# Expert chunks of one whole matrix: w1 or w3 in one load of 16 KB runs, multiplied 256 columns at a time

## The chip, the cores and the metric

The kernel runs on one core of one Trainium2 chip, in one launch. The metric is the device time in microseconds. Before the change three runs took 1033.55, 1036.56 and 1037.19 us, median 1036.56. A core has five engines that run their own instruction streams: TensorE (PE, with weight loads shown apart as PEld), VectorE (DVE), ScalarE (ACT), GpSimd (POOL) and SyncE (SP). Here SP issues nearly all loads from main memory; 16 DMA engines carry them out. All data is fp32; a matmul of fp32 operands shows as two records in the profile, one of fp32r operands (a rounded high part or its remainder) as one.

## The reference

256 tokens of width 1024 pass through two hybrid layers. The first ends in a mixture of 32 experts, the part that the change touches:

```
gl = h @ w_group + b_group;  g_idx = argmax(gl)              # 4 groups of 8 experts
el = (h @ w_expert) of that group + b_expert[g_idx]
vals, idx = top_k(softmax(el), 2); weights = g_w * vals / sum(vals)
for every expert e and the tokens x sent to it:
    y = (silu(x @ w1[e]) * (x @ w3[e])) @ w2[e]              # w1, w3: 1024 x 512, w2: 512 x 1024
out[token] += weight * y
```

Before it come two attention branches (Fox and differential) with gates, behind it a second hybrid layer with attention, a short convolution and their projections. Each of w1, w3 and w2 of one expert has 524288 numbers, 2.097 MB, so the experts together have 201.3 MB.

## The kernel before

**Stages.** The first layer's attention and projections take the span up to about 235 us, the experts 236 to 696 us, the second layer the rest.

**Experts.** An expert works on up to 64 slots for tokens. Four experts make a batch. A one-hot matrix (`PmR`) picks the tokens of a batch: for each of the eight blocks of 128 rows of the width, `gather(b, j)` multiplies the token rows (in a high and a low fp32r part, `XShR` and `XSlR`) by it, and VectorE copies the result out of the bank into `xe`, blocks 0 to 3 in one area and blocks 4 to 7 in another. Batch 0's gathers stand around expert 0, later ones are spread, two an expert. The products with w1 and w3 have the tokens as the stationary operand, 64 columns wide, so the array is split: output rows 0 to 63 of a bank take the first half of the 512 hidden columns (h = 0), rows 64 to 127 the other (h = 1). In the bank, columns 0 to 255 belong to w1 and 256 to 511 to w3. ScalarE applies Silu to the first, VectorE multiplies it by the second, TensorE transposes the result, and `down(e)` multiplies by w2, after the first half of the next expert. Every two experts `scatter` adds the outputs to the tokens in four banks.

**Loads.** A chunk of weights is 16 KB a partition, 2.097 MB. An expert has three: "a" has rows k = 0 to 3 of the eight that a partition holds, of w1 and of w3; "b" has rows 4 to 7 of both; "d" is w2. Each chunk is two DMAs of 1 MB with runs of 8 KB (line 246 builds them, line 839 in `load` issues them), and both raise the same semaphore, `landed`. The order of chunks is a0, b0, a1, d0, b1, a2, d1, b2 and so on; they go in turn into eight slots, five in `ring` and three in `arena`. Before it issues a load, SP waits in `released` until the slot's last chunk was used: for "a" by the semaphore `half`, which TensorE raises behind the first eight matmuls of an expert, for "b" and "d" by the bank's `full`. SP and its queue thus run as far ahead as TensorE frees slots.

**TensorE's order in an expert** (lines 1204 to 1257): chunk "a" in eight matmuls of 512 columns (four blocks, two halves; the 512 are 256 of w1 and 256 of w3, side by side in the chunk's two parts); `down` of the expert before; for expert 0 alone the gathers of blocks 4 to 7; at odd experts a scatter; chunk "b" in eight matmuls; two gathers of the next batch; the transposes. Before a block's matmul TensorE waits in `emptied` for VectorE's copy of that block, and before a gather in `may_write` for the bank that it writes.

**A branch.** The second 16 experts are written twice, in the two sides of a branch on `flag` (some expert has over 64 tokens, or not); TensorE reads the flag between experts 15 and 16. With these inputs it takes the side without overflow.

The names that the prediction uses: line 783 is the helper of every matmul, 839 the loads, 1302 to 1308 VectorE's helpers (1305 copies gathered tokens out), 2060 ScalarE's Silu, one an expert. In the changed file lines 783 and 839 are 782 and 838.

Of the kernel before, what the change touches and what calls it, by code (L numbers as in the profile page):

```python
# [22 lines left out]
SLOTS = 64  # L23
# [62 lines left out]
def bass_two_hybrid_blocks(nc, t, out):  # L86
    x_d, out_d = t["x"][0], out[0]
    with ExitStack() as ctx:
# [101 lines left out]
        ab = sm(224, 24)  # L190
# [49 lines left out]
        def expert_chunk(e, tag, what):  # L240

            if what == "d":
                w2 = t["w2"][0, e].rearrange("(g p c) n -> p g c n", g=2, c=2)
                return (tag, what, e), (w2[:, 0], w2[:, 1])
            k = 0 if what == "a" else 4
            return (tag, what, e), tuple(t[w][0, e].rearrange("(p k) n -> p k n", k=8)[:, k:k + 4, :] for w in ("w1", "w3"))

        def expert_chunks(tag):

# [47 lines left out]
        def space(nm):  # L297
            s = slot_of[nm]
            return ring[:, s * CH:s * CH + CH] if s < RING else area((60, 76, 102)[s - RING], CH)
# [482 lines left out]
        def mm(pe, o, l, r, start, stop):  # L782
            return pe.e.matmul(o, l, r, start=start, stop=stop)  # L783
# [362 lines left out]
        def experts_pe(pe, eng, r, P, S, lo, hi):  # L1146
# [4 lines left out]
            def gather(b, j):  # L1151
                u = P.of["g", r, b, j]
                may_write(pe, u)
                pe.wait_ge(S["select"], NB * g + b + 1)
                pe.wait_ge(s_xlow, 3)
                pe.wait_ge(s_xlow_dve, 1)
                for n in range(NT):
                    for x in (XShR, XSlR):
                        last = mm(pe, banks[u.bank][:, 0:256], x[:, n, j * 128:j * 128 + 128], PmR[:, b % 2, n, :],
                                  n == 0 and x is XShR, n == 1 and x is XSlR)  # L1160
                if b == 0 and j == 7:
                    last = slot_factors(0, banks[u.bank])
                last.then_inc(u.full, 1)
# [40 lines left out]
            for e in range(lo, hi):  # L1204
                b, k = divmod(e, EB)
                u = P.of["h", r, e]
                bank = banks[u.bank]
                for half in "ab":
                    may_write(pe, u)
                    pe.wait_ge(*landed[tag, half, e])  # L1210
                    w13 = space((tag, half, e)).rearrange("p (m k n) -> p m k n", m=2, k=4)
                    for j4 in range(4):
                        j = j4 + (4 if half == "b" else 0)
                        emptied(pe, P.of["g", r, b, j])
                        for h in range(2):
                            last = mm(pe, bank[64 * h:64 * h + 64, :].rearrange("p (m n) -> p m n", m=2),
                                      xe[b % 2][j // 4][:, j4, SLOTS * k:SLOTS * k + SLOTS], w13[:, :, j4, 256 * h:256 * h + 256],
                                      j == 0, j == 7)
                    if half == "a":
                        last.then_inc(S["half"], 1)  # L1220
                        if e:
                            down(e - 1)
                        if e == 0:
                            for j in range(4, 8):
                                gather(0, j)
                        if e > 2 and e % 2:
                            scatter((e - 3) // 2)
                    else:
                        last.then_inc(u.full, 1)
                if b + 1 < NB:  # L1230
                    gather(b + 1, 2 * k)
                    gather(b + 1, 2 * k + 1)
                if r in (0, 3) and e >= 28:
                    sp = P.of["spread", r, e - 28]
                    may_write(pe, sp)
                    pe.wait_ge(S["dg"], e - 27)
                    for i in range(4):
                        last = mm(pe, banks[sp.bank][:, 128 * i:128 * i + 128], ones[:, :], DG[i], True, True)
                    last.then_inc(sp.full, 1)
                if k == 2:  # L1240
                    w = P.of["w", r, b]
                    may_write(pe, w)
                    pe.wait_ge(s_identr, 1)
                    for p in range(2):
                        for n in range(NT):
                            last = mm(pe, banks[w.bank][:, 256 * p + 128 * n:256 * p + 128 * n + 128],
                                      PmR[:, b % 2, n, 128 * p:128 * p + 128], identR[:, :], True, True)
                    last.then_inc(w.full, 1)
                x = P.of["hT", r, e]
                may_write(pe, x)  # L1250
                emptied(pe, u)
                for c in range(2):
                    last = eng.transpose(banks[x.bank][:, 128 * c:128 * c + 128], Hb[e % 2][:, c:256:2], ident[:, :])  # L1253
                if k == 3 and b + 1 < NB:
                    last = slot_factors(b + 1, banks[x.bank])
                last.then_inc(x.full, 1)
# [1163 lines left out]
```

## Time and profile before

| | |
|---|---|
| runs | 1033.55, 1036.56, 1037.19 us |
| profiled execution | 1036.57 us, span 1034.8 us |
| mean granted TensorE clock | 0.985 of full |
| PE busy | 991.7 us (96%), 6369 matmul records |
| PEld busy | 697.8 us (67%) |
| DVE, ACT, POOL busy | 391.9, 377.1, 120.8 us |
| loads of expert weights | 192 DMAs of 1 MB (120 into ring, 72 into arena) |
| moved | 307.95 MB, mean 298 GB/s |

The span is the time from the first to the last instruction on the core. Busy PE is not PE at its peak: matmuls are pipelined, and their ends are modelled. Twice the same number of columns takes twice as long in the array, and the granted clock says at which share of its full clock the array runs in a stretch. An idle time has a releaser behind it: what ended it. "issue" stands where the profile shows nothing that was waited for. The rates by slice (40 equal parts of the span, 25.87 us each) show how full the queues are.

### The profile page before, as it was taken

How to read it: one execution, taken by the hardware profiler on the slowest of the kernel's cores; microseconds unless marked ns; L12 is line 12 of the kernel's file. 1: busy time of each engine (PE TensorE's matmuls, PEld its weight loads, DVE VectorE, ACT ScalarE, POOL GpSimd, SP SyncE). 2: the span in 40 equal slices, each digit the busy share in tenths (PEclk: the TensorE clock that was granted, in tenths of full speed). 3: DMA queues.
4: the chain of work that ended last, by engine and by line, in shares of the span. 5: the costliest groups of instructions: out<-in, count | busy, mean ns of one | idle time of the engine just before them, and what ended most of it. 6: DMA issues, size and time to landing. Idle time of an engine off the chain costs nothing.

```text
span 1034.8 us, 14930 instructions
## 1 busy us (share of the span) xinstructions
PE 991.7 (96%) x6369; PEld 697.8 (67%) x6369; DVE 391.9 (38%) x750; ACT 377.1 (36%) x612; POOL 120.8 (12%) x81
## 2 busy tenths in 40 slices
PE   7999999999999999979999999998999999999996
PEld 6988789975344434333344443348989999999995
DVE  3445446844222112121222211117334444774475
ACT  4445655641111111111111111216445555554443
POOL 1110021020000000000000000002321111341122
PEclk9999999999999999998999999999999999999998
DMA  8974386788999999999999999998545544445401
GB/s 270 347 277 147 125 319 252 284 324 337 421 422 421 419 421 421 421 420 420 422 421 421 421 421 421 421 404 297 201 166 186 187 167 167 163 164 198 148 1 41
DMA packets 84038, 307.95 MB, mean 298 GB/s; under 512 B 6609, under 2 KB 13170, under 8 KB 59386
## 3 DMA queue, kind: packets, MB, share of 16 engines
q1 hardware_dynamic: 80178, 302.16, 74.4%
q10 hardware_dynamic: 3784, 4.73, 1.4%
q8 instruction: 53, 0.87, 0.4%
q14 instruction: 23, 0.19, 0.1%
HBM read 305.82 MB, written 2.63 MB: 298 GB/s over the span
## 4 chain that ended last, share of the span: by engine, by line
PE 80%; DVE 6%; SPq 4%; DMA 3%; ACT 3%; issue 2%; POOL 1%; ACTq 0%; DVEq 0%
PE bank L783 78%; SPq L839 4%; DMA arena<-in_w 3%; DVE arena L1308 2%; DVE arena L1305 2%; ACT arena L2060 1%; PE bank L1253 1%; DVE wR L1302 1%; DMA arena<-in_rows 1%; PE bank L994 1%; DVE arena L1302 1%; POOL wR L2258 1%; ACT wR L1883 0%; DVE hTR L1302 0%; ACT arena L2113 0%
## 5 line engine op out<-in xcount | busy, mean ns | idle before, releaser
L783 PE MATMUL bank<-hTR,wR 128*128 128x256 f32 x2520 | 316.7, 286 | 4.5 <-DVE hTR L1308 1.3
L783 PEld LDWEIGHTS bank<-hTR,wR 128*128 128x128 f32 x2520 | 308.1, 193 | 8.5 <-issue 4.2
L783 PE MATMUL bank<-ring,arena 128*64 128x512 f32 (+2 forms) x1056 | 228.9, 600 | 8.0 <-issue 6.8
L1883 ACT ACTIVATE wR<-ring 128x1024 fp32r<-128x1024 f32 x161 | 168.3, 1054 | 111.1 <-PE bank L783 109.4
L1302 DVE TENSOR_TENSOR wR<-ring,wR 128x1024 fp32r<-128x1024 f32 x126 | 157.7, 1258 | 132.8 <-ACT wR L1883 132.5
L783 PE MATMUL bank<-arena 128*64 128x512 f32 (+7 forms) x778 | 165.5, 529 | 1.4 <-DVE small L1434 0.7
L783 PEld LDWEIGHTS bank<-ring,arena 128*64 128x64 f32 (+2 forms) x1056 | 69.9, 135 | 140.6 <-issue 136.9
L1308 DVE SCALAR_TENSOR_TENSOR arena<-bank,small,arena 128x256 f32<-128x256 f32 x32 | 15.5, 484 | 346.4 <-ACT arena L2060 346.4
L2031 ACT ACTIVATE arena<-bank,small 64x512 f32<-64x512 f32 x62 | 42.4, 684 | 280.7 <-PE bank L783 280.4
L2258 POOL TENSOR_TENSOR wR<-ring,wR 128x1024 fp32r<-128x1024 f32 x35 | 85.5, 2442 | 325.1 <-ACT wR L1883 325.1
L783 PEld LDWEIGHTS bank<-arena 128*64 128x64 f32 (+4 forms) x778 | 63.7, 148 | 85.5 <-issue 78.1
L2246 POOL TENSOR_TENSOR small<-small,mhalf 128x1 f32<-128x1 f32 (+1 forms) x12 | 7.2, 601 | 481.0 <-DVE small L1308 476.6
L783 PE MATMUL bank<-wR,hTR 128*128 128x512 f32 x192 | 45.2, 393 | 0.0
L2060 ACT ACTIVATE arena<-bank,small 128x256 f32<-128x256 f32 x32 | 15.2, 475 | 81.9 <-PE bank L783 81.9
L783 PEld LDWEIGHTS bank<-PmR,XShR 128*128 128x128 f32 x128 | 25.1, 196 | 24.2 <-issue 23.5
L783 PEld LDWEIGHTS bank<-wR,hTR 128*128 128x128 f32 x192 | 35.6, 188 | 8.1 <-issue 0.8
L783 PE MATMUL bank<-PmR,XShR 128*128 128x256 f32 x128 | 36.2, 314 | 0.4 <-DVE small L1494 0.3
L783 PE MATMUL bank<-PmR,XSlR 128*128 128x256 f32 x128 | 32.8, 287 | 0.0
L1305 DVE TENSOR_SCALAR arena<-bank,col 128x256 f32<-128x256 f32 x64 | 28.1, 476 | 4.8 <-PE bank L783 4.7
L1302 DVE TENSOR_TENSOR arena<-arena 128x512 f32<-128x512 f32 (+5 forms) x36 | 21.4, 603 | 10.8 <-ACT arena L2190 9.8
L1302 DVE TENSOR_TENSOR arena<-bank,arena 128x512 f32<-128x512 f32 (+2 forms) x30 | 19.6, 664 | 15.1 <-PE bank L783 12.8
L783 PEld LDWEIGHTS bank<-PmR,XSlR 128*128 128x128 f32 x128 | 25.2, 197 | 0.0
(209 smaller groups left out, 825.0 us busy)
## 6 DMA issues: line engine op xcount, KB each, us to landing
ring<-in_w SPq DMA_DIRECT2D x120, 1024.0 KB, 20.3
arena<-in_w SPq DMA_DIRECT2D x72, 1024.0 KB, 19.5
ring<-in_w_in SPq DMA_DIRECT2D x29, 2048.0 KB, 8.6
ring<-in_w_ada SPq DMA_DIRECT2D x6, 2048.0 KB, 7.9
ring<-in_w_o SPq DMA_DIRECT2D x2, 2048.0 KB, 12.3
ring<-in_w_o_attn SPq DMA_DIRECT2D x2, 2048.0 KB, 7.9
ring<-in_w_o_conv SPq DMA_DIRECT2D x2, 2048.0 KB, 8.6
ring<-in_w_out SPq DMA_DIRECT2D x2, 2048.0 KB, 8.1
```

Source lines behind the costliest of these rows:

```text
L783: return pe.e.matmul(o, l, r, start=start, stop=stop)
L839: e.e.dma_start(to[:, at_:at_ + k * n].rearrange("p (k n) -> p k n", k=k), part).then_inc(landed[nm][0], 16)
L994: last = eng.transpose(banks[u.bank][:, 128 * c:128 * c + 128], P[:, 128 * c:128 * c + 128], ident[:, :])
L1253: last = eng.transpose(banks[x.bank][:, 128 * c:128 * c + 128], Hb[e % 2][:, c:256:2], ident[:, :])
L1302: return eng.tensor_tensor(o, a, b, op)
L1305: return eng.tensor_scalar(o, a, s1, s2, op0) if op1 is None else eng.tensor_scalar(o, a, s1, s2, op0, op1)
L1308: return eng.scalar_tensor_tensor(out=o, in0=a, scalar=s, in1=b, op0=op0, op1=op1)
L1883: eng.activation(h, w, ACT.Copy).then_inc(s_high, 1)
L2031: last = eng.activation(Y[h0:h0 + 64, 512 * h:512 * h + 512], banks[u.bank][64 * h:64 * h + 64, :], ACT.Copy, scale=RW[64 * h:64 * h + 64, ...
L2060: eng.activation(Hb[e % 2], banks[u.bank][:, 0:256], ACT.Silu, scale=RW[:, e // EB % 2, e % EB, 1:2]).then_inc(S["silu"], 1)
L2246: eng.tensor_tensor(o, a, mhalf[:, 0:a.shape[1]], ALU.pow).then_inc(after, 1)
L2258: eng.tensor_tensor(l, pieces[i][1], h.bitcast(F32), ALU.subtract).then_inc(low[i][0], 1)
```

## The change

An expert's chunks "a" and "b" are now the whole w1 and the whole w3. A partition's eight rows of 512 numbers stand side by side in main memory, so its 16 KB are one run and the chunk is one DMA of 2 MB. TensorE multiplies chunk "a" for all eight blocks and then chunk "b" for all eight; a matmul takes 256 columns of one matrix and writes one half of the bank's columns. There are 32 such matmuls for an expert instead of 16 of twice the columns. The semaphore `half` is raised behind the whole of w1. The gathers of blocks 4 to 7 of batch 0 stand between blocks 3 and 4 of expert 0's w1, since these need them. The number of chunks, their size, slots and order stay, and w2 stays as it was.

```diff
@@ -242,8 +242,7 @@
-            k = 0 if what == "a" else 4
-            return (tag, what, e), tuple(t[w][0, e].rearrange("(p k) n -> p k n", k=8)[:, k:k + 4, :] for w in ("w1", "w3"))
+            return (tag, what, e), (t["w1" if what == "a" else "w3"][0, e].rearrange("(p k) n -> p k n", k=8),)
@@ -1205,24 +1204,23 @@
-                for half in "ab":
+                for m in range(2):
                     may_write(pe, u)
-                    pe.wait_ge(*landed[tag, half, e])
-                    w13 = space((tag, half, e)).rearrange("p (m k n) -> p m k n", m=2, k=4)
-                    for j4 in range(4):
-                        j = j4 + (4 if half == "b" else 0)
+                    pe.wait_ge(*landed[tag, "ab"[m], e])
+                    w13 = space((tag, "ab"[m], e)).rearrange("p (k n) -> p k n", k=8)
+                    for j in range(8):
+                        if e == 0 and m == 0 and j == 4:
+                            for j_ in range(4, 8):
+                                gather(0, j_)
                         emptied(pe, P.of["g", r, b, j])
                         for h in range(2):
-                            last = mm(pe, bank[64 * h:64 * h + 64, :].rearrange("p (m n) -> p m n", m=2),
-                                      xe[b % 2][j // 4][:, j4, SLOTS * k:SLOTS * k + SLOTS], w13[:, :, j4, 256 * h:256 * h + 256],
+                            last = mm(pe, bank[64 * h:64 * h + 64, 256 * m:256 * m + 256],
+                                      xe[b % 2][j // 4][:, j % 4, SLOTS * k:SLOTS * k + SLOTS], w13[:, j, 256 * h:256 * h + 256],
                                       j == 0, j == 7)
-                    if half == "a":
+                    if m == 0:
                         last.then_inc(S["half"], 1)
                         if e:
                             down(e - 1)
-                        if e == 0:
-                            for j in range(4, 8):
-                                gather(0, j)
                         if e > 2 and e % 2:
                             scatter((e - 3) // 2)
```

TensorE at the first expert, before. Rows are matmuls as issued, with the semaphores that they wait for (`ring6` and `ring1` are landed chunks, `free` is a bank copied out); 64x512 are the matmuls of w1 and w3, 128x256 the gathers, 64x2 the slot factors.

```order
L783 MATMUL bank<-arena 64x512 [waits free7]
L783 MATMUL bank<-arena 64x512
L783 MATMUL bank<-PmR,XShR 128x256
L783 MATMUL bank<-PmR,XSlR 128x256
L783 MATMUL bank<-arena,PmR 64x2 [waits weights]
L783 MATMUL bank<-arena,PmR 64x2 x15
L783 MATMUL bank<-ring,arena 64x512 [waits ring1]
L783 MATMUL bank<-ring,arena 64x512 x3
L783 MATMUL bank<-ring,arena 64x512 [waits free0]
```

The same place after the change.

```order
L782 MATMUL bank<-arena,PmR 64x2 [waits weights]
L782 MATMUL bank<-arena,PmR 64x2 x15
L782 MATMUL bank<-arena 64x256 x4
L782 MATMUL bank<-arena 64x256 [waits free0]
L782 MATMUL bank<-arena 64x256
L782 MATMUL bank<-arena 64x256 [waits free1]
L782 MATMUL bank<-arena 64x256
L782 MATMUL bank<-ring,arena 64x256 [waits ring1]
L782 MATMUL bank<-ring,arena 64x256 x15
```

Behind the slot factors now stand four more blocks of w1 (from `arena`), and only then the wait for the second chunk (`ring1`), whose sixteen matmuls are all w3. The waits for the copied blocks 6 and 7 (`free0`, `free1`) moved from w3's chunk into w1's.

SP's queue where the experts' loads begin, before: every chunk is two DMAs.

```order
L839 DMA arena<-in_w 128x2048 x2
L839 DMA ring<-in_w 128x2048 x2
L839 DMA arena<-in_w 128x2048 x2
L839 DMA ring<-in_w 128x2048 x4
L839 DMA arena<-in_w 128x2048 x2
```

The same loads after the change.

```order
L838 DMA arena<-in_w 128x4096
L838 DMA ring<-in_w 128x4096
L838 DMA arena<-in_w 128x4096
L838 DMA ring<-in_w 128x2048 x2
L838 DMA ring<-in_w 128x4096
```

The first three rows are w1 of expert 0, w3 of expert 0 and w1 of expert 1, one DMA each; the pair behind them is w2 of expert 0, unchanged.

## Rows read from the trace of the kernel before

**Rows 1.** The page, section 2: GB/s in 40 slices of the span.

```profile
GB/s 270 347 277 147 125 319 252 284 324 337 421 422 421 419 421 421 421 420 420 422 421 421 421 421 421 421 404 297 201 166 186 187 167 167 163 164 198 148 1 41
```

**Rows 2.** Busy time by stretch: engines' busy us (instructions), clock, DMA share, GB/s.

```profile
240.00:260.00 20.00, 19.56 (x127) 8.95 (x127) 6.75 (x26) 2.02 (x4) 0.00 (x0) 1.00 0.91 350
300.00:440.00 140.00, 136.53 (x702) 56.83 (x700) 25.59 (x58) 25.02 (x42) 0.00 (x0) 1.00 1.01 421
686.00:700.00 14.00, 11.65 (x60) 5.78 (x59) 1.60 (x3) 3.74 (x7) 0.00 (x0) 1.00 1.03 388
```

**Rows 3.** ScalarE's timeline, Silu (start us, us, what, idle before); experts 5, 9, 15, 16.

```profile
318.97 0.47 ACT L2060 ACTIVATE arena<-bank,small 128x256 f32<-128x256 f32 x1 [4.25 <-PE bank L783]
...
374.53 0.48 ACT L2060 ACTIVATE arena<-bank,small 128x256 f32<-128x256 f32 x1 [4.25 <-PE bank L783]
...
457.67 0.47 ACT L2060 ACTIVATE arena<-bank,small 128x256 f32<-128x256 f32 x1 [4.24 <-PE bank L783]
479.93 0.47 ACT L2060 ACTIVATE arena<-bank,small 128x256 f32<-128x256 f32 x1 [0.88 <-PE bank L783]
```

**Rows 4.** TensorE's timeline behind the branch, and a stretch of 2 us there.

```profile
466.89 6.12 PE L783 MATMUL bank<-ring,arena 128*64 128x512 f32 x16 [6.25 <-issue]
...
468.00:470.00 2.00, 2.00 (x8) 0.51 (x6) 0.00 (x0) 0.00 (x0) 0.00 (x0) 0.50 1.01 422
```

**Rows 5.** TensorE's timeline near the end; then one row of the waits, 250 to 700.

```profile
666.21 3.65 PE L783 MATMUL bank<-arena 128*64 128x512 f32 x16 [0.18 <-DMA arena<-in_w]
671.08 3.65 PE L783 MATMUL bank<-ring,arena 128*64 128x512 f32 x16 [1.22 <-DMA ring<-in_w]
...
681.12 3.65 PE L783 MATMUL bank<-arena 128*64 128x512 f32 x16 [0.52 <-DMA arena<-in_w]
...
PE bank L783 <- DMA arena<-in_w: 0.7, 2, 0.5
```

**Rows 6.** The DMA view of 300 to 440 us.

```profile
DMA packets 8088, 58.92 MB, mean 421 GB/s; under 512 B 902, under 2 KB 902, under 8 KB 902
```

**Rows 7.** Timelines of TensorE, VectorE and SP at expert 0.

```profile
240.26 3.65 PE L783 MATMUL bank<-arena 128*64 128x512 f32 x16
...
242.61 0.75 DVE L1302 TENSOR_TENSOR PmR<-kpack,arena 128x256 fp32r<-128x256 f32 x2
...
243.95 0.80 SPq L839 DMA_DIRECT2D arena<-in_w  x2
244.62 0.48 DVE L1305 TENSOR_SCALAR arena<-bank,col 128x256 f32<-128x256 f32 x1 [1.26 <-PE bank L783]
...
247.26 3.63 PE L783 MATMUL bank<-ring,arena 128*64 128x512 f32 x16
```

**Rows 8.** Timeline of TensorE's weight loads, full clock, then half.

```profile
499.94 0.14 PEld L783 LDWEIGHTS bank<-ring,arena 128*64 128x64 f32 x2 [0.29 <-issue]
...
505.95 0.14 PEld L783 LDWEIGHTS bank<-ring,arena 128*64 128x64 f32 x2 [0.28 <-issue]
...
467.80 0.24 PEld L783 LDWEIGHTS bank<-ring,arena 128*64 128x64 f32 x2 [0.61 <-issue]
...
471.21 0.24 PEld L783 LDWEIGHTS bank<-ring,arena 128*64 128x64 f32 x2 [0.62 <-issue]
```

**Rows 9.** TensorE's timeline: slot factors, two columns each, and what follows.

```profile
524.01 1.10 PE L783 MATMUL bank<-arena,PmR 128*64 128x2 f32 x32
524.96 6.21 PE L783 MATMUL bank<-ring,arena 128*64 128x512 f32 x28
```

**Rows 10.** TensorE's timeline of gathers: at half clock, then at full.

```profile
237.13 0.42 PE L783 MATMUL bank<-PmR,XSlR 128*128 128x256 f32 x1
...
239.48 0.41 PE L783 MATMUL bank<-PmR,XShR 128*128 128x256 f32 x1
...
251.05 0.28 PE L783 MATMUL bank<-PmR,XSlR 128*128 128x256 f32 x1
...
251.76 0.28 PE L783 MATMUL bank<-PmR,XSlR 128*128 128x256 f32 x1
```

## The prediction

> **What bounds the kernel now.** I read the slices of the page first, because the change touches one stage only: the 32 experts. From slice 10 to slice 25 the load rate stands at 419 to 422 GB/s [rows 1]. The second view was the busy time by stretch: between 300 and 440 us the 16 DMA engines are full (share 1.01, 421 GB/s), and TensorE is busy for 136.53 of 140 us [rows 2]. So both look like the bound, and the question is which of them is late. The third view gives TensorE's pace: ScalarE's Silu, one an expert, starts at 318.97 us for expert 5 and at 374.53 us for expert 9, so four experts take 55.56 us, 13.89 us each [rows 3]. An expert has three matrices of 2.097 MB; at 421 GB/s its 6.291 MB take 14.94 us. TensorE is thus the faster of the two by 1.05 us an expert, and lives on the chunks that were already in the buffers when it began.
>
> Two things hold the balance until the end. At expert 16 TensorE loses about 8.4 us: from 457.67 to 479.93 us it takes 22.26 us [rows 3], where the mean is 13.89. There TensorE goes through the branch on the flag and stands idle for 6.25 us without a releaser, and then works for some 5 us at a granted clock of 0.50, the 1.2 GHz level [rows 4]. That stop gives the loads 8.4 us. The fourth view, TensorE's timeline near the end, shows where the reserve is used up: it waits for a chunk 0.18 us at 666.21, 1.22 us at 671.08 and 0.52 us at 681.12, 1.92 us together; the view of waits for 250 to 700 us has these three and no other for a load, the two on arena as its row of 0.7 us [rows 5]. So the two finish in a dead heat: if loads become faster, the stage gains at most 1.92 us, since TensorE is then the bound; if TensorE becomes slower, all but about 1.9 us of it is paid.
>
> **The change part by part, the loads.** The bytes stay: 192 DMAs of 1 MB become 64 of 2 MB (w1, w3) and 64 of 1 MB (w2), in the same order of chunks, into the same slots. In 300 to 440 us 8088 packets carry 58.92 MB, 902 of them under 512 B; the other 7186 carry 8.2 KB each, which is the length of a run in the source [rows 6]. So runs are not cut, and a run of 16 KB should be one packet of 16 KB. What that is worth follows from two sizes: with runs of 2 KB (the w_in_2 loads at 686 to 700 us) a full queue moves 388 GB/s [rows 2], with 8 KB 421. Per engine that is 84.5 and 311.3 ns a packet, so 6144 more bytes cost 226.8 ns; twice 8 KB is then 311.3 + 302.4 = 613.7 ns, a rate of 427 GB/s. That is an estimate from the two rates. On the 134.2 MB of w1 and w3 it takes 318.8 us down to 314.3, 4.5 us less of queue time. The lower bound is nothing (the rate stays at 421).
>
> **The first expert.** Only there does the order of TensorE change: the gathers of blocks 4 to 7 move from behind the eight matmuls of chunk "a" to the middle of the sixteen of w1. Before, "a" runs from 240.26 and its slot is free for a new load at 243.95; the second half starts at 247.26 [rows 7]. After, blocks 0 to 3 of w1 take half of its 3.6 us, to 242.1; four gather records of 0.12 us make one block, so gathers 4 and 5 run to 243.1; gather 6 needs the bank of gather 4, which VectorE copies out only behind its two PmR writes (242.61 plus 0.75, so 243.4) and in 0.48 us [rows 7], hence 243.9; gathers 6 and 7 end at 244.9, the slot factors (32 short records) take 0.95 us [rows 9], so blocks 4 to 7 of w1 start at 245.85. Eight pairs of half a pair's 429.3 ns [rows 8] take them to 247.6, sixteen take w3 to 251.0. Before, the eight pairs from 247.26 ended at 250.7. That is **+0.3 us** on TensorE. Its bounds are 0 (the copies come as fast as the gathers) and +1 us (each of the four copies of 0.48 us waited for in part). The slot of chunk "a" comes free at 247.6 instead of 243.95. For the loads this matters less than it looks: between 240 and 260 us the queue moves 350 GB/s instead of 421 [rows 2], so it stands empty 3.4 us in sum, waiting for slots. Afterwards it is empty from about 245 (my reading of where the issued loads end) to 248.7, one us behind the issue, 3.7 us, and then full, as a chunk lasts 5 us and the slot of w3 is free at 251.0. The loads lose 0.3 us of their 4.5.
>
> **The matmuls.** An fp32 matmul shows as two records, and two records for the two halves of the columns (64 wide) run side by side. Each expert has 16 matmuls of 512 columns for w1 and w3, 32 records, 16 pairs; afterwards 32 matmuls of 256, 64 records, 32 pairs. The columns streamed are the same, the fixed cost of a pair is paid twice as often. Its size: between the weight loads at 499.94 and 505.95 us lie 14 pairs, 429.3 ns each; at the half clock four pairs from 467.80 to 471.21 take 852.5 ns each, so the array's own time at full clock is 426.3 [rows 8]. The fixed part is 3.0 ns a pair. Sixteen more pairs in 32 experts: 512 x 3.0 ns = **+1.5 us**. The added weight loads (64 columns, two a pair) lie under the running pair: with only two columns to stream, 32 records with their loads take 0.95 us from 524.01 to 524.96, 29.7 ns each [rows 9], so the two loads of a pair need under 60 ns of the 213 that a pair of 256 columns lasts. If that cover went, every one of the 1024 added records would cost up to 29.7 ns, 30.4 us. The other bound from a near row is the gather: 128 wide, 256 columns, at full clock 0.71 us for six records (118 ns), at half clock 2.35 us for eleven (213.6, so 106.8 at full), hence 11.5 ns fixed a record [rows 10]. I take 3.0 ns a pair, because that row is the same code, width and engine mode with twice the columns, and nothing in it grows when the stream gets shorter.
>
> The Trainium skill, "TensorE: Matmul & The Clock Gate" (Part 1, on 56 against 53.3 ns), gives a fixed cost of about 2.5 ns a warm matmul. By that rule the 1024 added records would cost 2.6 us, not 1.5. The rows show 3.0 ns for two records, lower than the rule, and no row here shows 256 columns in this mode.
>
> All other parts cost nothing: the Silu and the product read w1's and w3's halves of the bank when both are complete, as before; the slot of chunk "a" is free after half of the matmuls, as before, except in expert 0; the SP queue issues 64 DMAs fewer.
>
> **The sum.** The profiled execution took 1036.57 us around a span of 1034.8, and the median of the runs is 1036.56, so both are the same base. 1036.57 + 0.3 (first expert) + 1.5 (pairs) = 1038.4, less the 1.92 us of waits for chunks, which end when the loads are 4.2 us earlier: **1036.4 us**. What follows the experts hangs on their last matmul and moves with it.
>
> **The rivals.** *Each short matmul pays.* One mechanism: the change of weights is not hidden behind a stream of only 256 columns. The cost is then as in the gather, 11.5 ns a record: 64 x 11.5 - 32 x 1.5 = 0.69 us an expert, 22.0 us in all, less 1.92 and plus 0.3: 1057.0 us, slower. It decides from about 8.3 ns a pair: 1024 short pairs x (8.3 - 3.0) = 5.4 us, which with the forecast is 0.5% above before. For it: the gather has just this number of columns. Against it: the second tile works while the first one changes its weights, and the 32-record row shows loads at 29.7 ns. Chance 0.15.
>
> The Trainium skill's page "TensorEngine Tiling (Array Packing)", section Instruction Overhead, puts some 60 cycles on each matmul and warns against spending them on small sizes. Added to each of 1024 records as 25 ns, an estimate from that page at 2.4 GHz, this would give 25.6 us, 1060 in all; the 29.7 ns row shows such a floor for two columns, but as a floor, not as an addition. This belongs to the rival just told.
>
> *The branch takes longer.* The 6.25 us of idle time at the branch [rows 4] fall in full DMA queues; packets of double length before TensorE's own could double it: 1036.4 + 6.25 = 1042.7, slower. For it: the share is 1.00 and more there. Against it: no row shows that the stop is made of waits for packets of the loads, and those of w2 and the total of bytes in the queue stay as they are. Chance 0.07.
>
> *The loads still end last.* The long runs bring nothing, the queue is 0.3 us later and the waits stay: about 1036.9, no change. TensorE's 1.8 us are then covered by the 1.92 of waits. Chance 0.12.
>
> *The branch takes less.* If the stop at the branch hangs on where in the loads it falls, it can shrink as well. Its whole length is the bound: 1036.4 - 6.25 = 1030.1. Chance 0.05.
>
> **How the numbers follow.** Forecast 0.61, own range 1033.5 to 1040. A measurement of this kernel tells about 0.5% (5.2 us) from no change. The forecast and the third rival lie within that (0.73, of which I leave 0.02 to faster and 0.03 to slower by the spread of 1033.55 to 1037.19 that the runs have), the first two rivals are slower (0.22), the last is faster (0.05). That gives faster 0.07, same 0.68, slower 0.25. The range is 1031.5 to 1046: it leaves out the price of the gather and the end of the branch rival below.
>
> **What would show it.** Right: weight loads of w1 and w3 in pairs 0.214 to 0.217 us apart; 13.9 to 13.95 us an expert; loads at 425 to 428 GB/s with runs of 16 KB; no wait for a chunk after 660 us; expert 0's Silu at 251 to 252 us. Wrong: pairs 0.23 us apart or more (first rival); an idle time at expert 16 far from 6.25 us; waits for chunks that stay or grow, which would mean that the loads became slower by their size and not faster.

## The result and the profile after

The changed kernel takes 1031.81 us (median of 7 runs, 1030.85 to 1033.19) against 1034.61 us for the kernel before (7 runs, 1032.9 to 1037.19, the three told above among them). The ratio is 0.9973, 95% interval 0.9962 to 0.9983: 2.8 us faster, 0.27%, which is inside the 0.5% that I had called no change. Two repeats below give 0.9987 and 0.9980.

The profiled execution of the changed kernel took 1032.23 us, its span 1030.4 us, 4.4 us less than in the one before. It is best read by stages. First the pace of the experts: ScalarE's timeline after the change, the Silu of experts 0, 15, 16, 29 and 31 (start us, us, what, idle before).

```profile
248.07 0.47 ACT L2058 ACTIVATE arena<-bank,small 128x256 f32<-128x256 f32 x1 [3.32 <-PE bank L782]
...
455.37 0.47 ACT L2058 ACTIVATE arena<-bank,small 128x256 f32<-128x256 f32 x1 [4.27 <-PE bank L782]
477.90 0.48 ACT L2058 ACTIVATE arena<-bank,small 128x256 f32<-128x256 f32 x1 [0.89 <-PE bank L782]
...
659.38 0.47 ACT L2058 ACTIVATE arena<-bank,small 128x256 f32<-128x256 f32 x1 [4.27 <-PE bank L782]
...
686.43 0.47 ACT L2058 ACTIVATE arena<-bank,small 128x256 f32<-128x256 f32 x1 [4.26 <-PE bank L782]
```

From expert 0 to 15 an expert takes 207.30 / 15 = 13.820 us; before, 13.782 (250.94 to 457.67). The stretch with the branch takes 22.53 us instead of 22.26 [rows 3], its idle time is 6.51 us instead of 6.25 [rows 4], and half clock follows as before (granted clock 0.52 from 465 to 470 us):

```profile
464.85 6.12 PE L782 MATMUL bank<-ring,arena 128*64 128x256 f32 x32 [6.51 <-issue]
```

The ledger of the two profiled executions, by such starts (the first gather of TensorE marks the start of the stage):

| stretch | before us | after us | difference |
|---|---|---|---|
| start of span to first gather | 236.75 | 233.69 | -3.06 |
| first gather to Silu 0 | 14.19 | 14.38 | +0.19 |
| Silu 0 to Silu 15 | 206.73 | 207.30 | +0.57 |
| Silu 15 to Silu 16, the branch | 22.26 | 22.53 | +0.27 |
| Silu 16 to Silu 29 | 180.96 | 181.48 | +0.52 |
| Silu 29 to Silu 31 | 29.59 | 27.05 | -2.54 |
| Silu 31 to end of span | 344.32 | 343.97 | -0.35 |

The change is in rows 2 to 6. They give -1.0 us in all. The -3.06 us lie ahead of the experts, where the change touches only a few loads that SP issues in advance; the experiments take that up.

The row that gains is the one with the waits for chunks. TensorE's timeline after the change at experts 30 and 31, to be held against [rows 5]:

```profile
660.86 3.67 PE L782 MATMUL bank<-ring,arena 128*64 128x256 f32 x32
664.36 3.60 PE L782 MATMUL bank<-arena 128*64 128x512 f32 x16
667.79 3.62 PE L782 MATMUL bank<-ring,arena 128*64 128x256 f32 x32
...
677.14 3.60 PE L782 MATMUL bank<-arena 128*64 128x512 f32 x16
```

No row has a DMA as its releaser: all waits for chunks are gone. The loads did become faster. The stretch 300 to 440 us after the change (busy us by engine, clock, DMA share, GB/s), and the packets of the same stretch:

```profile
300.00:440.00 140.00, 136.53 (x1028) 79.98 (x1024) 25.61 (x58) 24.91 (x42) 0.00 (x0) 1.00 1.01 425
...
DMA packets 5405, 59.49 MB, mean 425 GB/s; under 512 B 602, under 2 KB 602, under 8 KB 602
```

Against [rows 2, 6]: 425 GB/s instead of 421, and 4803 large packets of 12.4 KB on average instead of 7186 of 8.2 KB, since a partition now gets two runs of 16 KB and two of 8 KB an expert (12.3 KB on average). TensorE has 1028 matmul records instead of 702 for the same busy time.

The weight loads of a w1 after the change are one unbroken row:

```profile
507.41 3.22 PEld L782 LDWEIGHTS bank<-arena 128*64 128x64 f32 x32
```

Their 0.14 us each overlap into one busy stretch, where [rows 8] had 0.28 us of idle time after every pair. It looks tight and is not: the pace of 13.820 us says that 16 more pairs cost 38 ns, 2.4 ns each.

Last, the first expert (TensorE and SP after the change), to be held against [rows 7]:

```profile
236.92 2.32 PE L782 MATMUL bank<-arena 128*64 128x256 f32 x16
239.18 0.39 PE L782 MATMUL bank<-PmR,XShR 128*128 128x256 f32 x1
...
242.65 1.93 PE L782 MATMUL bank<-arena 128*64 128x256 f32 x16
244.40 3.62 PE L782 MATMUL bank<-ring,arena 128*64 128x256 f32 x32
244.61 0.33 SPq L838 DMA_DIRECT2D arena<-in_w  x1
```

The gathers stand between the halves of w1, and the first slot is free 10.92 us behind the first gather instead of 7.20 (243.95 - 236.75).

### The profile page after: what moved, and what is told of

Same layout as the page of the kernel before. It is cut to its first block, busy times and chain, and to the rows that moved or that the text cites. A ratio compares the mean times of both kernels' runs of the same rounds, so it can differ in the third digit from the quotient of the medians.

```text
span 1030.4 us, 16914 instructions
## 1 busy us (share of the span) xinstructions
PE 988.3 (96%) x7393; PEld 767.3 (74%) x7393; DVE 392.5 (38%) x750; ACT 377.1 (37%) x612; POOL 121.8 (12%) x81
## 4 chain that ended last, share of the span: by engine, by line
PE 85%; DVE 7%; ACT 4%; issue 2%; POOL 1%; DMA 1%; SPq 0%; ACTq 0%; DVEq 0%
PE bank L782 82%; DVE arena L1306 3%; DVE arena L1303 2%; PE bank L1251 1%; ACT arena L2058 1%; DVE wR L1300 1%; DMA arena<-in_rows 1%; PE bank L993 1%; DVE arena L1300 1%; ACT wR L1881 1%; POOL wR L2256 1%; ACT arena L2088 0%; DVE hTR L1300 0%; ACT arena L2086 0%; ACT arena L2111 0%
## 5 line engine op out<-in xcount | busy, mean ns | idle before, releaser
L782 PE MATMUL bank<-ring,arena 128*64 128x256 f32 (+3 forms) x1680 | 229.6, 439 | 7.1 <-issue 7.1
L782 PEld LDWEIGHTS bank<-ring,arena 128*64 128x64 f32 (+2 forms) x1680 | 115.3, 137 | 103.1 <-issue 59.7
L782 PE MATMUL bank<-arena 128*64 128x256 f32 (+7 forms) x1178 | 166.5, 406 | 0.7 <-DVE small L1432 0.7
L782 PEld LDWEIGHTS bank<-arena 128*64 128x64 f32 (+3 forms) x1178 | 92.3, 144 | 62.4 <-issue 28.3
## 6 DMA issues: line engine op xcount, KB each, us to landing
ring<-in_w_o SPq DMA_DIRECT2D x2, 2048.0 KB, 12.4
```

## The experiments

Each ratio is to the kernel before, measured on the same chip in the same job. "Silu 0 to 31" is the experts' stage in the profiled execution of that kernel. In the unaltered kernels it repeats to 0.1 us where the times of whole runs scatter by 5, so most verdicts rest on it; every other kernel has one profiled execution.

| kernel | time us | before us | ratio, 95% interval | first gather | to Silu 0 | Silu 0 to 31 | to end |
|---|---|---|---|---|---|---|---|
| before | 1034.61 | | | 236.75 | 14.19 | 439.54 | 344.32 |
| before again | 1034.85 | 1034.85 | 1.0001 [0.9988, 1.0014] | 235.37 | 12.96 | 439.56 | 344.41 |
| changed | 1031.81 | 1034.61 | 0.9973 [0.9962, 0.9983] | 233.69 | 14.38 | 438.36 | 343.97 |
| changed again | 1033.91 | 1035.02 | 0.9987 [0.9975, 1.0] | 237.13 | 15.07 | 438.32 | 344.28 |
| changed, third | 1033.06 | 1034.85 | 0.998 [0.9967, 0.9993] | 235.74 | 15.09 | 438.40 | 343.97 |
| short matmuls alone | 1035.69 | 1035.02 | 1.0004 [0.999, 1.0017] | 234.76 | 14.33 | 440.85 | 343.96 |
| 8 KB runs, two DMAs | 1036.59 | 1035.02 | 1.0016 [1.0002, 1.0029] | 235.41 | 14.38 | 441.98 | 343.73 |
| 8 KB runs, one DMA | 1036.87 | 1034.85 | 1.002 [1.0008, 1.0033] | 234.53 | 14.41 | 441.83 | 343.93 |
| before, less w2 | 1030.7 | 1034.44 | 0.996 [0.9946, 0.9975] | 235.20 | 12.95 | 436.82 | 343.83 |
| before, branch at end | 1039.39 | 1034.44 | 1.0048 [1.003, 1.0066] | 237.12 | 14.95 | 439.06 | 350.77 |
| changed, branch at end | 1039.12 | 1034.44 | 1.0045 [1.0027, 1.0062] | 235.17 | 13.24 | 437.76 | 350.43 |
| the same, no filler | 1032.9 | 1034.85 | 0.9979 [0.9966, 0.9993] | 234.97 | 13.26 | 437.33 | 344.34 |
| 128 columns | 1038.69 | 1034.44 | 1.0026 [1.0011, 1.0042] | 237.18 | 14.98 | 440.99 | 344.95 |

**Short matmuls alone.** The kernel before with its loads, and the products cut in two.

```diff
-                            last = mm(pe, bank[64 * h:64 * h + 64, :].rearrange("p (m n) -> p m n", m=2), ..., w13[:, :, j4, 256 * h:256 * h + 256],
+                        for m in range(2):
+                            for h in range(2):
+                                last = mm(pe, bank[64 * h:64 * h + 64, 256 * m:256 * m + 256], ..., w13[:, m, j4, 256 * h:256 * h + 256],
+                                          j == 0 and m == 0, j == 7 and m == 1)
```

> The kernel before with its loads (8 KB runs, two DMAs a chunk), but every product with w1 and w3 as two matmuls of 256 columns. Theory (the fixed part of a pair is paid twice, and the load stream still ends last): Silu to Silu 0.04 to 0.05 us an expert longer than before (13.78 to 13.82 from expert 0 to 15); queue at 421 GB/s; the waits for chunks near the end shrink from 2.6 us (by starts) to about 1.3, so the time is 0 to +0.5 us against before. Rival (the long runs are not what made the changed kernel faster, it is the short matmuls or the order): about 1032, 2 to 3 us below before. If each short record paid as in the gather: +20 us.

Silu 0 and Silu 15 of this kernel:

```profile
249.09 0.47 ACT L2061 ACTIVATE arena<-bank,small 128x256 f32<-128x256 f32 x1 [1.59 <-PE bank L783]
...
456.36 0.47 ACT L2061 ACTIVATE arena<-bank,small 128x256 f32<-128x256 f32 x1 [4.28 <-PE bank L783]
```

13.818 us an expert, the same as in the changed kernel. So the slower pace is all of it the short matmuls. The stage is 1.3 us longer than before, and no gain appears. The expected drop of the waits to 1.3 us did not come: Silu 29 to 31 takes 29.82 us, 0.2 more than before, since here the loads arrived 1.5 us later behind the first gather too (expert 30's w2 is used from 680.59 on, 445.83 us behind it; before, from 681.12 on, 444.37 behind). In the 397 us that begin 3 us behind the first gather the queue moved 165.39 MB instead of 165.64, which is 0.6 us of the 1.5. Whether it moved less because TensorE freed its slots later is not shown, nor where the rest of the 1.5 us lies.

**8 KB runs under the changed kernel, in two DMAs.**

```diff
-            return (tag, what, e), (t["w1" if what == "a" else "w3"][0, e].rearrange("(p k) n -> p k n", k=8),)
+            w13 = t["w1" if what == "a" else "w3"][0, e].rearrange("(p k) n -> p k n", k=8)
+            return (tag, what, e), (w13[:, 0:4, :], w13[:, 4:8, :])
```

> The changed kernel, but each whole w1 or w3 comes in two DMAs of 1 MB with runs of 8 KB, as long as before. Theory (run length gives the rate): queue back from 425 to 421 GB/s in the middle of the stage, about 600 packets a 58.9 MB more small ones as before, waits of 1 to 3 us for chunks come back at experts 30 and 31, time 2 to 3 us above the changed kernel, that is about as before or 0.5 us above it. Rival (what was gained lies before the experts or in the first expert): the time stays at that of the changed kernel.

Its waits for loads and its rate:

```profile
PE bank L783 <- DMA ring<-in_w: 2.6, 2, 1.4
...
PE bank L783 <- DMA arena<-in_w: 1.6, 3, 0.8
...
300.00:440.00 140.00, 136.53 (x1029) 80.10 (x1027) 25.62 (x58) 25.51 (x43) 0.00 (x0) 1.00 1.01 420
```

The rate is back at 420, the waits are 4.2 us, more than the 1 to 3 expected, and the stage is 3.6 us longer than in the changed kernel (441.98 against 438.36); in time it is 2.7 us above the changed kernel of the same job, as expected. So the theory holds. The stretch with the branch is shorter here, 20.82 us instead of 22.53 (20.97 in the next experiment), with less idle time and a granted clock of 0.73 instead of 0.52 in the 5 us behind it:

```profile
465.93 5.04 PE L783 MATMUL bank<-ring,arena 128*64 128x256 f32 x32 [5.87 <-issue]
```

The loads take these 1.7 us back: Silu 16 to 31 is 5.3 us longer than in the changed kernel. What makes the stop vary is not shown.

**8 KB runs in one DMA.** The count of DMAs as changed, the length of runs as before. The DMA takes two groups of four rows for a partition that lie apart in memory, so the products pair other rows of w1 and w3 with the tokens than the reference does; the work is the same.

```diff
+            w13 = t["w1" if what == "a" else "w3"][0, e].rearrange("(g p k) n -> p g (k n)", g=2, k=4)
+            return (tag, what, e), (w13,)
```

> The changed kernel with each whole w1 or w3 in one DMA of 2 MB, but in runs of 8 KB: the DMA takes two separate groups of four rows for every partition, so the rows that meet in a product are other ones than in the reference (the computation's values change, its shape and work do not). It has the change's number of DMAs and the old run length. Theory (run length gives the rate): 421 to 422 GB/s and 2 to 3 us slower than the changed kernel. Rival (the number of DMAs gives it, each with its own small packets): 424 to 425 GB/s and the time of the changed kernel.

```profile
300.00:440.00 140.00, 136.52 (x1028) 80.10 (x1026) 25.61 (x58) 25.52 (x43) 0.00 (x0) 1.00 1.01 421
...
DMA packets 7774, 58.89 MB, mean 421 GB/s; under 512 B 595, under 2 KB 595, under 8 KB 595
```

It has as few small packets as the changed kernel (595 against 602) and yet the old rate, and the stage of the two DMAs (441.83 against 441.98 us). So the length of a run makes the 425, and neither the number of DMAs nor the small packets with them.

**16 KB runs in two DMAs of 64 partitions.**

```diff
+            w13 = t["w1" if what == "a" else "w3"][0, e].rearrange("(p k) n -> p k n", k=8)
+            return (tag, what, e), (w13[0:64], w13[64:128])
```

> The changed kernel, but each whole w1 or w3 comes in two DMAs of 64 partitions each, runs of 16 KB as in the change. Theory (run length, not the number of DMAs): 425 GB/s, time as the changed kernel within 1 us. Rival (the number of DMAs, each with its own small packets, sets the rate): about 421 to 423 GB/s and 1 to 3 us slower than the changed kernel.

It took 1454.38 us, ratio 1.3989 [1.393, 1.4049]. This experiment failed at its question, since it changed something larger. Its middle stretch:

```profile
300.00:440.00 140.00, 90.63 (x534) 47.73 (x534) 12.94 (x31) 10.14 (x17) 0.00 (x0) 0.79 1.01 228
```

All 16 engines are busy (share 1.01) and move 228 GB/s, and TensorE is busy for 90.63 of 140 us. The last section comes back to it.

**Less of w2.** The kernel before, but from expert 16 on the second half of w2 is not loaded and old weights are used in its place.

```diff
-                return (tag, what, e), (w2[:, 0], w2[:, 1])
+                return (tag, what, e), (w2[:, 0],) if e >= 16 else (w2[:, 0], w2[:, 1])
```

> The kernel before, but from expert 16 on only the first half of w2 is loaded (the rest of the slot holds old weights), 16.8 MB less, so the load stream ends some 40 us earlier. Everything else as before. Theory (before, TensorE waited for chunks only at experts 30 and 31, 2.6 us by starts): those waits go and nothing else, Silu 29 to Silu 31 takes 27.0 us instead of 29.6, time 2.6 us below before. Rival (waits for loads are hidden elsewhere, or full queues slow the branch): more than 4 us below, with less than 6.25 us of idle time at the branch.

Silu 29 and Silu 31:

```profile
657.99 0.47 ACT L2060 ACTIVATE arena<-bank,small 128x256 f32<-128x256 f32 x1 [4.25 <-PE bank L783]
...
684.97 0.47 ACT L2060 ACTIVATE arena<-bank,small 128x256 f32<-128x256 f32 x1 [4.24 <-PE bank L783]
```

26.98 us, as expected, and every other stretch of the stage as before: the waits at the end were worth 2.6 us, and there were no others. The pace up to expert 15 (13.778) and the branch (22.23) did not move. The time fell by 3.7 us (interval 2.6 to 5.6), more than the stage's 2.7, which lies just inside the interval.

**The branch at the end**, in the kernel before and in the changed one. TensorE's experts 16 to 31 stand once, ahead of the branch.

```diff
-            with eng.If(eng.value_load(flag[0:1, 0:1]) > SLOTS):
-                experts_pe(pe, eng, 0, PB, S, NE // 2, NE)
+            flag_value = eng.value_load(flag[0:1, 0:1])
+            experts_pe(pe, eng, 0, PB, S, NE // 2, NE)
+            known = dict(pe.known)
+            with eng.If(flag_value > SLOTS):
                 pe.wait_ge(s_ofold, NT)
...
             with eng.Else():
-                experts_pe(pe, eng, 0, PB, S, NE // 2, NE)
                 warm(pe, banks[7], 26)
```

> The kernel before, but TensorE's experts 16 to 31 stand once, ahead of the branch; the branch is taken behind the last scatter, where TensorE has only filler matmuls. Theory (the dead heat: the stop at the branch, 8.4 us, is lent by the loads): TensorE passes expert 16 in 13.4 us instead of 22.3, then waits about 8 us more for chunks before the end of the stage; the stage ends as before within 1 us, time 0 to +3 us, as the stop comes again behind the experts partly uncovered. Rival (TensorE is the bound and the loads have room): 6 to 8 us faster.

> The same move of the branch in the changed kernel. Theory (its loads end some 2 to 3 us earlier than TensorE needs them): the stage ends 2 to 3 us earlier than in the changed kernel and is then bound by the loads, of which the stop behind the experts can take back up to 3; time -3 to +1 us against the changed kernel. Rival (the stop can be had back whole): 8 us faster.

The kernel before with the branch at its end: Silu 15 and 16; then its waits of TensorE.

```profile
458.76 0.47 ACT L2061 ACTIVATE arena<-bank,small 128x256 f32<-128x256 f32 x1 [4.26 <-PE bank L783]
472.13 0.48 ACT L2061 ACTIVATE arena<-bank,small 128x256 f32<-128x256 f32 x1 [0.88 <-PE bank L783]
...
PE bank L783 <- issue: 5.6, 2, 5.1
PE bank L783 <- DMA ring<-in_w: 5.5, 6, 1.3
PE bank L783 <- DMA arena<-in_w: 2.8, 4, 1.5
```

Expert 16 takes 13.37 us instead of 22.3, and the stage is only 0.5 us shorter (439.06): 8.4 of the 8.9 us came back behind expert 16, as ten waits for chunks (8.3 us shown). That is the dead heat of the prediction, shown. In the changed kernel the same move shortens the stage by 0.6 us (437.76 against 438.36), not by the 2 to 3 expected. Both kernels then pay behind the experts, 6.5 us more from Silu 31 to the end, where I had expected at most 3. The next row, of the kernel before with the branch at its end, shows why: the fillers wait behind the stop.

```profile
708.05 8.43 PE L783 MATMUL bank<-ident 128*128 128x128 f32 x52 [5.05 <-issue]
```

**The same without filler**, in the changed kernel: the 26 filler matmuls (52 records) of the Else side are left out.

```diff
-            with eng.Else():
-                warm(pe, banks[7], 26)
```

> The changed kernel with TensorE's branch behind the last scatter, and without the 52 records of filler matmuls that stood there, so that the stop at the branch falls into the time that they filled. Theory: the stage ends 1.7 us earlier as in the run with the filler (loads are the bound again), the tail behind expert 31's Silu is 346 to 347 us instead of 344 to 344.3 (half clock for some 5 us at the start of the second layer, no queueing behind fillers), so 0 to +1 us against the changed kernel, where the version with the filler was 6 us slower. Rival (the stop costs the same wherever it stands): +5 us or more. If nothing of the half clock shows: 1.7 us faster than the changed kernel.

```profile
703.61 3.81 PE L986 MATMUL bank<-ident,arena 128*128 128x128 f32 x16 [6.25 <-ACT arena L2089]
```

The stop has vanished into the 6.25 us for which TensorE waits for ScalarE's norm (in the changed kernel the fillers fill 5.96 us of this time), and the tail is 344.34 us, 0.3 more than in the changed kernel. The stage is 1.0 us shorter. The time is the changed kernel's, 1032.9 against 1033.06 us in the same job. So this version is 2.0 us faster than the kernel before (interval 0.7 to 3.5), and cannot be told from the changed one.

**128 columns.** The changed kernel with 64 matmuls an expert for w1 and w3.

```diff
-                        for h in range(2):
-                            last = mm(pe, bank[64 * h:64 * h + 64, 256 * m:256 * m + 256], ..., w13[:, j, 256 * h:256 * h + 256],
+                        for q in (0, 128):
+                            for h in range(2):
+                                last = mm(pe, bank[64 * h:64 * h + 64, 256 * m + q:256 * m + q + 128], ..., w13[:, j, 256 * h + q:256 * h + q + 128],
```

> The changed kernel with its w1 and w3 products cut once more, 64 matmuls of 128 columns an expert, 64 pairs. Theory (2.4 to 3 ns a pair, weight loads hidden as long as 60 ns of loading fit under 107 of streaming): 32 more pairs an expert, 0.08 to 0.10 us, 13.90 us an expert, 2.5 to 3 us slower than the changed kernel. Rival (a short stream stops covering the loads; a load takes 137 ns from start to end, longer than the 107 ns of a pair): pairs 137 ns apart or more, 64 x 30 ns = 1.9 us an expert, 60 us slower.

```profile
252.16 0.47 ACT L2060 ACTIVATE arena<-bank,small 128x256 f32<-128x256 f32 x1 [3.38 <-PE bank L782]
...
460.65 0.47 ACT L2060 ACTIVATE arena<-bank,small 128x256 f32<-128x256 f32 x1 [4.32 <-PE bank L782]
```

13.899 us an expert: 32 more pairs cost 79 ns, 2.5 ns each, as the 16 before them did. The stage is 2.6 us longer. Even streams of 128 columns cover their weight loads, although a load is recorded at 138 ns on average and a pair lasts about 110 (213 / 2 + 2.5, an estimate from [rows 8]).

**Both kernels again.**

> The changed kernel once more, unaltered. Theory (the 3.06 us that its profile shows ahead of the experts are scatter of the granted clock, since nothing is changed there): ratio to before 0.997 to 0.999 and a stretch ahead of the first gather that can lie anywhere between 233.5 and 237 us. Rival (something systematic ahead of the experts): again 233.7 us, and 3 us or more below before.

> The changed kernel, unaltered, beside the next one on the same chip. Theory (what the traces show between expert 0's and expert 31's Silu, 1.2 us, is the change's whole effect, the rest is scatter ahead of it): ratio 0.998 to 0.9995, Silu 0 to Silu 31 438.3 to 438.4 us. Rival (3 us are systematic): 0.9965 to 0.9975.

> The kernel before, unaltered, as a control of the comparison: ratio 0.9985 to 1.0015, Silu 0 to Silu 31 439.5 us within 0.3, and a first gather anywhere between 233.5 and 237.5 us. If its first gather lies at 236 to 237 us once more while the changed kernel's third lies at 233 to 235, the stretch ahead of the experts is not scatter.

The stage repeats: 439.54 and 439.56 us before, 438.36, 438.32 and 438.40 changed. What lies ahead of it does not: the first gather came at 233.69, 237.13 and 235.74 us in the changed kernel, at 236.75 and 235.37 before. So the 3.06 us of the first two profiles are scatter, and most of it can be placed: the kernel before ran at half clock for a part of 18 to 25 us and of 72 to 87 us (mean granted clock 0.76 and 0.89), the changed one did not. These are the two stretches, first before, then changed:

```profile
18.00:25.00 7.00, 7.00 (x49) 7.00 (x48) 3.24 (x5) 2.45 (x4) 1.93 (x1) 0.76 0.72 203
72.00:87.00 15.00, 14.27 (x101) 13.18 (x100) 7.34 (x22) 8.13 (x16) 2.39 (x1) 0.89 0.65 235
...
18.00:25.00 7.00, 7.00 (x60) 7.00 (x60) 4.26 (x6) 3.25 (x4) 2.40 (x1) 1.00 0.66 191
72.00:87.00 15.00, 14.27 (x114) 12.68 (x112) 7.96 (x24) 8.01 (x18) 1.95 (x1) 1.00 0.65 237
```

The changed kernel gains about 1.5 and 1.3 us there (by the starts of ScalarE's instructions behind them), and both lie ahead of the first load of expert weights (185.86 and 182.82 us). The same holds for the stretch to Silu 0 (12.96 and 14.19 before), where the half clock falls ahead of the first gathers or onto them. The control has a ratio of 1.0001.

## Why the prediction came out as it did

The direction, the mechanism and the range held: 1031.81 lies in 1031.5 to 1046, near its low end; the forecast of 1036.4 was 4.6 us too high. Of these 4.6 us, 1.96 are the base. I built the sum on an execution of 1036.57 us, and the median of three runs agreed with it by chance; more runs give 1034.4 to 1035.0. Against its own base the forecast was -0.2 us and the measurement is -2.8, -1.1 and -1.8 us. A range of 14.5 us around so small an effect was not hard to hold. Of the signs of being right, 13.93 us an expert (5 to 9), 425 GB/s and no wait for a chunk after 660 us came as said; expert 0's Silu came at 248.07 in one profile and at 252.20 and 250.83 in the repeats, which scatter more than the sign allowed.

**Right: who is the bound.** The dead heat was read off three short waits, and the run with less of w2 and the two with the branch at the end show it from both sides: without waits TensorE gains 2.6 us, and without the stop it gains 0.5.

**Mis-sized: the waits for chunks, "the 1.92 us of waits".** I summed what the timeline gives as idle before an instruction. The timeline ends a group of matmuls with the modelled end of the last one, which overlaps the start of the next when they follow each other. The right measure is from start to start: in [rows 5], 666.21 to 671.08 is 4.87 us for a group that takes 3.43 us undisturbed, 1.44 us of loss beside 1.22 shown. The three together are 2.46 us (0.34, 1.44 and 0.68), and 0.14 us more lies in the steps right behind the second and the third; removing them gave 2.54 (changed kernel, which has 0.08 us of longer pairs in this stretch) and 2.61 (less of w2).

**Right: the pairs.** Forecast 3.0 ns a pair, 1.5 us; measured 2.4 ns, 1.2 us. The rival of 22 us, each short matmul paying as in the gather, is dead: 128 columns pay no more either. The rule of about 2.5 ns a matmul in the Trainium skill, "TensorE: Matmul & The Clock Gate", comes out as 2.4 to 2.5 ns a pair of records here, and not a record. The 60 cycles of overhead in the Trainium skill, "TensorEngine Tiling (Array Packing)", Instruction Overhead, do not add here. Added to each record they would have made the experiment with 128 columns 50 us slower (an estimate from that page: 2048 records more, 25 ns each at 2.4 GHz), and its stage became 2.6 us longer. The page's own example, one column that lasts as long as 60, reads as a floor, and the 29.7 ns of a record of two columns [rows 9] agree with that.

**Right: the rate.** The extrapolation from runs of 2 and 8 KB gave 427 GB/s for w1 and w3, 425 with w2's share at 421; measured 424 to 425 in the long stretches with 16 KB runs.

**Right: the first expert, "+0.3 us".** The stretch from the first gather to Silu 0 scatters by 2 us with the half clock, but four profiles have none in it: 12.96 and 12.95 us in the order of before (before again, less w2), 13.24 and 13.26 us in the changed order (the two with the branch at the end). That is 0.3 us, as worked out. The stretch around it in before again, then in the changed kernel with the branch at its end (granted clock 1.00 in both):

```profile
233.40:248.30 14.90, 14.22 (x109) 8.55 (x109) 7.49 (x30) 1.81 (x3) 0.00 (x0) 1.00 0.98 396
...
233.00:250.00 17.00, 15.54 (x149) 11.92 (x150) 8.60 (x33) 2.49 (x4) 0.00 (x0) 1.00 0.82 329
```

**Mis-sized: the first expert's slot, "The loads lose 0.3 us".** The slot came free 3.7 us later, as worked out. The next 30 us of the queue, from 3 us behind the first gather on, in the kernel before and in the changed one:

```profile
239.75:269.75 30.00, 29.21 (x174) 13.02 (x175) 8.69 (x30) 3.81 (x6) 0.00 (x0) 1.00 0.94 375
```

```profile
236.69:266.69 30.00, 29.17 (x250) 18.51 (x251) 8.12 (x29) 3.81 (x6) 0.00 (x0) 0.98 0.88 361
```

Empty time is 30 x (1 - 375/421) = 3.3 us before and 30 x (1 - 361/425) = 4.5 us after, 1.2 us more, not 0.3. At equal runs of 8 KB the two kernels that differ in this order show 372 and 358 GB/s, 1.0 us, and their stages differ by 1.1 us (440.85, 441.98). The half clock moves these rates too, but two profiles without it give the same: 391 GB/s in before again and 377 in the changed kernel with the branch at its end, 1.2 us. So a quarter of what the long runs bring is lost at the start. It costs nothing here, because TensorE is the bound afterwards. How much the loads have in hand can be seen with the branch at the end: the stage shortens by 0.6 and 1.0 us before waits stop it.

**The other rivals.** In the changed kernel the branch took at most 0.3 us longer and not less; it did take 1.3 to 1.7 us less in the two kernels with runs of 8 KB and short matmuls in the changed order, where the loads were the bound and nothing was won. The loads do not end last. What the stop costs was read a little low: 8.4 us against the mean of the experts, but expert 16 without a branch takes 13.37 us, so it is 8.9.

**The account.** The stage between Silu 0 and Silu 31 changed by -1.2 us: +1.2 to +1.4 for the pairs and the branch, -2.5 for the waits. With the 0.3 us of the first expert the traces give -0.9 us from the first gather on. The three comparisons average -1.9 us. The intervals of the second and the third hold -0.9 (-2.6 to 0, -3.4 to -0.7), that of the first does not (-3.9 to -1.8). The traces don't show where the 1.0 us between them would be; that stays open. From Silu 31 to the end the changed kernel's three profiles are 0.3 us shorter on average than the two of before, but kernels that share this part scatter by as much (343.73 to 344.41).

## What to carry to other kernels

When two resources finish together, a faster one gains only the waits of the other: find these waits first, and measure them from start to start against an undisturbed repeat. A fixed cost per instruction is to be taken from a row of the same array layout; the gather's 11.5 ns a record belonged to another one and would have been nearly ten times too much (1.2 ns a record measured). And the base of a sum should be the median of many runs, with the scatter of the untouched stretches known before a difference of 3 us is explained.

## What the runs showed of the hardware

Loads into 64 partitions: two DMAs of 1 MB with runs of 16 KB, one to partitions 0 to 63 and one to 64 to 127, fill the 16 engines (share 1.01) and move only 228 GB/s with w2's loads among them. If w2 still moved at 421, those for w1 and w3 ran at about 185 GB/s, an estimate (2/3 of the bytes: 1/228 = 0.667/185 + 0.333/421). The kernel became 40% slower. I had expected no difference. The Trainium skill, "DMA: Bandwidth & Descriptors" (Rules for kernel authors), advises one transfer of 128 partitions over two of half, on the ground that both share the same engines; the run agrees with the advice. Its engines were full at little over half the rate, which sharing alone would not give; what holds them is not shown by this run.

Runs of 8 KB move 421 GB/s and runs of 16 KB 425 with w2's 8 KB runs among them, so even at this size the length of a run is worth 1%. The same DMA of 2 MB with runs of 8 KB moved 421, so it is not the size of the DMA.
